# Value tiles as halves: six of eight between the rounds of branch A, two in its sequence, with six value buffers

## The reference, cut to what matters

```python
z = h @ p['w_in']                       # 1024 -> 6944
za = z[..., :SHIFT_W]                   # branch A
zb = z[..., SHIFT_W:SHIFT_W + RET_W]    # branch B: q, k, v, gate
...
def step(S, inp):                       # branch A, token by token
    sk = jnp.einsum('bhvk,bhk->bhv', S, kk_t)
    S = S * w_t[:, :, None, :] - sk[..., None] * b_t[:, :, None, :] + v_t[..., None] * k_t[:, :, None, :]
    return S, jnp.einsum('bhvk,bhk->bhv', S, r_t)
...
q, k, v, gate = jnp.split(zb, [B_QK, 2 * B_QK, 2 * B_QK + B_V], axis=-1)   # v: 8 tiles of 128 columns
```

## Time and profile before

| | |
|---|---|
| runs of the kernel | 1261.36, 1262.67, 1263.44 us; median 1262.67 |
| the profiled execution | 1262.1 us, of it span 1260.3 |
| mean granted TensorE clock | 0.995 |
| PE busy | 1217.3 us (97%), 12056 matmuls |
| PEld, DVE, ACT, POOL busy | 1154.1, 855.5, 558.0, 151.1 us |
| rounds of layer 0 and 1 | 108.3 to 157.8 us, 727.6 to 777.1 us |
| sequence of layer 0 and 1 | 157.8 to 194.5 us, 777.1 to 816.8 us |

### The profile page before, as it was taken

The page is one execution under the profiler, slowest core; times in us unless marked ns, Lnnn a source line. Parts: engine busy times, 40 slices in busy tenths (PEclk is TensorE's granted clock), DMA queues, the critical chain, the costliest instruction groups (busy, mean ns, idle before and its releaser), DMA issues.

```text
span 1260.3 us, 27905 instructions
## 1 busy us (share of the span) xinstructions
PE 1217.3 (97%) x12056; PEld 1154.1 (92%) x12056; DVE 855.5 (68%) x1469; ACT 558.0 (44%) x848; POOL 151.1 (12%) x168
## 2 busy tenths in 40 slices
PE   6999899999999999999999998999999999999996
PEld 5999788999998999999988987889999989999996
DVE  4887558888767766654488965588878576666433
ACT  5553345455445433344354544345463463333432
POOL 0004565100000000000000071920100000000000
PEclk9999999999999999999999999999999999999998
DMA  6433144555453644544434323264544535445441
GB/s 224 137 114 124 55 115 161 200 157 167 135 160 110 207 153 153 149 149 151 150 100 134 120 87 103 73 226 159 161 150 141 161 120 167 150 143 158 149 149 63
DMA packets 51466, 179.13 MB, mean 142 GB/s; under 512 B 6288, under 2 KB 7568, under 8 KB 50064
## 3 DMA queue, kind: packets, MB, share of 16 engines
q1 hardware_dynamic: 42576, 153.77, 39.1%
q10 hardware_dynamic: 8768, 23.58, 5.4%
HBM read 166.18 MB, written 8.53 MB: 139 GB/s over the span
## 4 chain that ended last, share of the span: by engine, by line
PE 86%; DVE 8%; ACT 4%; issue 1%; DMA 0%; ACTq 0%; SPq 0%; DVEq 0%
PE dense L1409 54%; PE core L1409 31%; DVE w_lo L923 2%; ACT w_hi L599 1%; DVE x L983 1%; DVE y_out L981 1%; ACT h_hi L605 1%; DMA x<-x_t 0%; DVE h_lo L1356 0%; DVE bonus L1052 0%; DVE tmp L1038 0%; DVE bonus L1048 0%; ACT sq_mixed L606 0%; PE core L1629 0%; DVE s_ga L1347 0%
## 5 line engine op out<-in xcount | busy, mean ns | idle before, releaser
L923 DVE TENSOR_TENSOR w_lo<-w_raw,w_hi 128x1024 fp32r<-128x1024 f32 x282 | 352.1, 1252 | 215.7 <-ACT w_hi L599 214.7
L599 ACT ACTIVATE w_hi<-w_raw 128x1024 fp32r<-128x1024 f32 x281 | 296.5, 1057 | 429.6 <-PE dense L1409 288.2
L1409 PE MATMUL dense<-h_hi,w_hi 128*128 128x320 f32 x1296 | 413.0, 319 | 16.7 <-DVE w_lo L923 11.7
L1409 PE MATMUL dense<-h_hi,w_lo 128*128 128x320 f32 x1296 | 401.7, 310 | 0.0
L1409 PE MATMUL dense<-h_lo,w_hi 128*128 128x320 f32 x1296 | 396.7, 311 | 0.4 <-DVE h_lo L927 0.4
L1409 PEld LDWEIGHTS dense<-h_hi,w_hi 128*128 128x128 f32 x1296 | 244.8, 189 | 34.9 <-issue 26.5
L1409 PEld LDWEIGHTS dense<-h_lo,w_hi 128*128 128x128 f32 x1296 | 243.3, 189 | 2.7 <-DVE h_lo L927 1.3
L1409 PEld LDWEIGHTS dense<-h_hi,w_lo 128*128 128x128 f32 x1296 | 245.0, 189 | 0.2
L1409 PE MATMUL core<-h_hi,w_hi 128*128 128x320 f32 x416 | 129.1, 310 | 0.5 <-DVE w_lo L923 0.5
L1409 PE MATMUL core<-h_hi,w_lo 128*128 128x320 f32 x416 | 128.5, 309 | 0.0
L1409 PE MATMUL core<-h_lo,w_hi 128*128 128x320 f32 x416 | 128.5, 309 | 0.0
(11 more groups left out here) (307 smaller groups left out, 1987.0 us busy)
## 6 DMA issues: line engine op xcount, KB each, us to landing
w_raw<-wts SPq DMA_DIRECT2D x282, 512.0 KB, 3.5
ret_t<-ret_t ACTq DMA_DIRECT2D x16, 256.0 KB, 4.1
ret_s<-ret_t ACTq DMA_DIRECT2D x16, 256.0 KB, 4.4
ret_rest<-ret_d ACTq DMA_DIRECT2D x2, 1536.0 KB, 8.7
qk_rot<-qk_raw SPq DMA_DIRECT2D x8, 320.0 KB, 6.4
dmask<-rconst ACTq DMA_DIRECT2D x2, 1152.0 KB, 5.5
s_st<-wkv_st ACTq DMA_DIRECT2D x2, 1024.0 KB, 5.0
wkv_s<-s_st ACTq DMA_DIRECT2D x2, 1024.0 KB, 4.2
```

The source lines that it names most:

```text
L599: act.activation(w_hi[n % RING][:, :], w_raw[n % RING][:, :], ACT.Copy).then_inc(hi_ready.sem, 1)
L923: dve.tensor_tensor(w_lo[r][:, :], w_raw[r][:, :], w_hi[r][:, :].bitcast(F32), ALU.subtract).then_inc(low_made.sem, 1)
L1409: return pe.matmul(out, lhsT, rhs, start=start, stop=stop)
```

## The change

Before, four value tiles stand in the rounds, each as three pieces of 3, 3 and 2 blocks, at twelve places; four whole tiles stand in the sequence. After, six tiles stand at the same twelve places as halves of 4 and 4 blocks, and the last two as four halves at the four places of the sequence. All matmuls are the same ones; 48 of them a layer move from the sequence to the rounds. The buffers `v_f` grow from four to six; one lies where `v_tok` begins, so the turns take tile 4 first. The low parts made in the rounds go from four to six, those behind `ys 0`, `ys 1`, `ys 2`, `w 3` from 2, 1, 1, 1 to 1, 1, 0, 1.

```diff
-THIRDS = ((0, 3), (3, 6), (6, 8))
-PIECE_AT = {at: (n // 3, THIRDS[n % 3]) for n, at in enumerate((2, 5, 8, 12, 16, 20, 24, 28, 32, 37, 42, 48))}
-LOW_AT = {10: 1, 18: 2, 30: 3, 42: 4}
+HALVES = ((0, 4), (4, 8))
+PIECE_AT = {at: (n // 2, HALVES[n % 2]) for n, at in enumerate((2, 5, 8, 12, 16, 20, 24, 28, 32, 37, 42, 48))}
+LOW_AT = {6: 1, 13: 2, 21: 3, 29: 4, 37: 5, 45: 6}
...
-FILL_AFTER = {("w", 0): [("turn", 0)], ("u", 0): [("turn", 1)], ("ys", 0): [("tile", 4)], ("w", 1): [("turn", 2)],
...
-LOWS_AFTER = {("ys", 0): (5, 6), ("ys", 1): (7,), ("ys", 2): (8,), ("w", 3): (9,)}
+TURNS = (4, 0, 1, 2, 3, 5, 6, 7)
+FILL_AFTER = {("w", 0): [("turn", 0)], ("u", 0): [("turn", 1)], ("ys", 0): [("half", 12)], ("w", 1): [("turn", 2)],
+              ("u", 1): [("turn", 3)], ("ys", 1): [("half", 13)], ("w", 2): [("turn", 4)], ("ys", 2): [("half", 14)],
+              ("as3", SAMPLE): [("turn", 5)], ("w", 3): [("half", 15)], ("w", SAMPLE): [("turn", 6)], ("u", 3): [("turn", 7)]}
+LOWS_AFTER = {("ys", 0): (7,), ("ys", 1): (8,), ("w", 3): (9,)}
...
-HIGH_AFTER = {("as0", SAMPLE): 4, ("u", 2): 5}
+HIGH_AFTER = {("u", 2): 6}
...
-        v_f = [at("v_f0", 32, T), at("v_f1", 33.25, T), at("v_f2", 34.5, T), at("v_f3", 48, T)]
+        v_f = [at("v_f0", 32, T), at("v_f1", 33.25, T), at("v_f2", 34.5, T), at("v_f3", 124, T),
+               at("v_f4", 38, T), at("v_f5", 48, T)]
...
-                        act.wait_ge(*v_turned(layer, j - T_V - len(v_f) + 1))
+                        act.wait_ge(*v_turned(layer, TURNS.index(j - T_V - len(v_f)) + 1))
...
-                    if h:
-                        pe.wait_ge(*v_tok_ready(layer, h))
+                    if n:
+                        pe.wait_ge(*v_tok_ready(layer, n))
...
-                        if what == "tile":
-                            plain(T_V + i, T_V + i)
+                        if what == "turn":
+                            turn(i)
                         else:
-                            turn(i)
+                            piece(T_V + i // 2, *HALVES[i % 2])
```

More of the change, by code:

```diff
@@ L106 @@
 V_FIRST = max(j for j, _ in PIECE_AT.values()) + 1
-FILL_AFTER = {("w", 0): [("turn", 0)], ("u", 0): [("turn", 1)], ("ys", 0): [("tile", 4)], ("w", 1): [("turn", 2)],
-              ("u", 1): [("turn", 3)], ("ys", 1): [("tile", 5)], ("w", 2): [("turn", 4)], ("ys", 2): [("tile", 6)],
-              ("as3", SAMPLE): [("turn", 5)], ("w", 3): [("tile", 7)], ("w", SAMPLE): [("turn", 6)], ("u", 3): [("turn", 7)]}
-LOWS_AFTER = {("ys", 0): (5, 6), ("ys", 1): (7,), ("ys", 2): (8,), ("w", 3): (9,)}
+TURNS = (4, 0, 1, 2, 3, 5, 6, 7)
[3 more added lines that the diff above has]
+LOWS_AFTER = {("ys", 0): (7,), ("ys", 1): (8,), ("w", 3): (9,)}
 TAIL = [("gate", 0), ("s", 0), ("mean", 0), ("mean", 1), ("s", 1), ("gate", 1), ("s", 2), ("mean", 2), ("mean", 3), ("gate", 2),
@@ L735, in _, with turned_values @@
                         values(T_V + PIECE_AT[i][0])
-                def turned_values(h):
-                    act.wait_ge(*v_turned(layer, h + 1))
+                def turned_values(n):
+                    h = TURNS[n]
+                    act.wait_ge(*v_turned(layer, n + 1))
                     vt = v_tok[:, 0:2048].rearrange("p (b c) -> p b c", b=2)
@@ L767, in _ @@
                     for what, i in FILL_AFTER.get(step, []):
-                        if what == "tile":
-                            values(T_V + i)
-                        else:
+                        if what == "turn":
                             turned_values(i)
+                        elif HALVES[i % 2][1] == KT:
+                            values(T_V + i // 2)
                     if step in HIGH_AFTER:
@@ L1620, in _, with turn @@
                         piece(T_V + PIECE_AT[i][0], *PIECE_AT[i][1])
-                def turn(h):
+                def turn(n):
+                    h = TURNS[n]
                     pe.wait_ge(*v_feat(layer, h + 1))
-                    if h:
-                        pe.wait_ge(*v_tok_ready(layer, h))
+                    if n:
+                        pe.wait_ge(*v_tok_ready(layer, n))
                     f = v_f[h % len(v_f)]
```

## The result

The changed kernel takes 1268.16 us (median of 5 runs, 1264.48 to 1269.09) against 1262.67: a ratio of 1.0041, 95% interval [1.0029, 1.0053]. In a second series on another chip it was 1264.75 us (10 runs, 1262.62 to 1270.45) against 1261.74, ratio 1.0025 [1.0011, 1.0039]. It is slower by 3.0 to 5.5 us; forecast were 6.5 us less, and the time lies outside the range given.

The account below looks back on a forecast made before the run. The prediction took the pace of instruction pages, 3.87 us each, to bound the rounds where pages hold little dense work. Its terms, -3.2 - 3.3 - 0.8 + 0.8 = -6.5 us, gave a median of 1256.2 us, range 1252.5 to 1261.5.

Parts of the forecast that it names:

- Pages bound the rounds: Rounds: where pages of about 126 matmuls hold little dense work, they come every 3.87 us and PE waits for them.
- the rival of no page effect: Rounds: pages aren't the bound and the issue waits stay, so no change, 1262.7 us; chance 0.12.
- The gain of 1.6 us a layer: Rounds of both layers: with 48 matmuls moved in, page waits fall from 3.5 to 1.9 us; -3.2 us for both.
- The late page, -3.3: Layer 1's sequence: the wait for a late instruction page and the half-clock stretch behind it go; -3.3 us.
- The first rival: Sequence of either layer: a page still stands behind the swaps, so the -3.3 is missing, 1259.5 us; chance 0.22.
- "Nothing else": Rest of the kernel: switches stay 16 a layer and the buffers' places add no wait; 0 us, tails included.
- The sequence: Sequence with half the filler: 7.06 us of work leaves each layer's, new waits cost 0.4 us a layer, +0.8 together.
- Waits for DVE: Sequence: up to 0.2 us behind `ys 1` and 0.2 for the samples' `w` copy, 0.4 a layer.
- The wait for `m_sq`: Rounds: PE's 0.4 us wait for ACT's result should be gone; part of the -0.8 us term for result waits.
- The slower rival: Sequences run out of pages: two new late pages besides the old, 3.3 us each, 1266.1 us; chance 0.08.
- the four terms: Page waits in the rounds -3.2, late page -3.3, result waits in the rounds -0.8, sequence with half the filler +0.8 us.

Follow-up runs that it names:

- the small loads: Changed kernel with the weight loads issued within the rounds (tiles 27 to 32 of each layer) bringing 16 rows instead of 128: 1260.00 us, ratio to before 0.9982.
- b_small_loads: Kernel before with the weight loads issued within the rounds (tiles 27 to 30 of each layer) bringing 16 rows instead of 128: 1263.04 us, ratio 1.0002.
- a_again: The changed kernel run once more with nothing altered, for a second profile: ratio 1.0025 to the kernel before.
- a_third: The changed kernel with nothing altered, for a third profile: 1268.31 us, one execution.

## Why the prediction was wrong, step by step

**Pages bound the rounds: right.** The rounds of layer 0 grew by 5.1 us for 7.06 us of moved work, as forecast, and spreading the pieces took further page waits away. PE's own rows show less of it than the sum had: 2.2 us of "issue" in layer 0's rounds now, 2.5 before, where under 2 was forecast, and all its idle time there fell from 3.8 to 2.8 us (49.50 - 45.71, 53.90 - 51.06). The clearest sign is the stops at page ends there, from the last start in one page to the first in the next: those over 0.1 us sum to 3.9 and 4.6 us in the two profiles of the kernel before, and to 2.2 to 2.7 in the four after. The Trainium skill (Runtime: NRT & Kernel Launch, "Instruction fetch mechanics") holds that fetching is hidden. PE's stop of 0.65 us at 762.74, behind a fetch that began 2.6 us late, speaks against it again, so the rival of no page effect falls.

**The gain of 1.6 us a layer: wrong in layer 1, by 2.7 us.** This is the step that failed most clearly. I wrote that the change moves 48 matmuls, and costed these. But a tile that moves into the rounds brings its weight load with it: six loads there instead of four. I had shown the move on SP myself, and counted it only as a gain at the swaps. The loads now come about every 9 us, which is two pages, and in layer 1 in such a phase that every second page is fetched behind one: PE's waits for pages there rose from 2.4 to 3.5 us, where 1.9 was forecast, and fell to 0.9 with the small loads. The page of the earlier trace rows would not have told me, for it comes as late without a full load ahead of it (b_small_loads). What would have is the one fetch of before's rounds that a load did hold, at 773.47 us, 2.7 us late, just as a load of 512 KB ends.

**The late page, -3.3: wrong, by 3.4 us.** Two errors. The 3.3 was one execution's: in the other three profiles with before's order the sequence of layer 1 took 41.8 to 43.0 us, not 44.7, so that the mean of the four has 1 us to give against the shortest, not 3.3. And a stall stayed in three profiles of four. The two loads behind the swaps no longer hold the page, but the last load ahead of them and the swaps themselves now do, and PE comes into the swaps with the page still to be fetched. The first rival had said this, with a chance of 0.22.

**"Nothing else": wrong, 2.8 us in the tails.** I followed what stands behind the swaps on SP, and not who waits for them: POOL's eight rotations, ACT behind these, and then `dmask` on top of the tail's weight load. All of it hangs on the end of the rounds, which now comes 4.4 us further behind their start. About 1.1 of the 2.2 us in layer 0 is the clock drop, in two of the four profiles; in layer 1, a_again and a_third wait 1.2 and 1.0 us for `sq_a`.

**The sequence: right in the sum for layer 0, by luck, since two errors cancel.** Waits for DVE were forecast at 0.4 us a layer. In layer 0 PE now waits 0.8 us for `w_st`, 0.7 for `y_a` behind `ys 1` and 0.5 for `wu_s`, where it waited 0.2 for `w_st` and 0.4 for `v_tok`:

```profile
178.87 0.31 PE L1412 MATMUL dense<-h_hi,w_lo 128*128 128x320 f32 x1
179.86 0.27 PE L1412 MATMUL dense<-v_st,tok 64*64 64x64 f32 x2 [0.68 <-DVE y_a L1170]
```

That is 1.4 us more. Page waits of 0.9 to 1.7 us in the same stretch of the kernel before went to 0.5 and less, which I had not counted. The wait for `m_sq` went, as forecast.

**The slower rival** (three late pages in the sequences, 1266.1) gave nearly the right time by mostly the wrong place. One of its stalls was there.

**The range** was narrower than its own terms. Added up from 1262.7, the bounds of the four terms run from 1250.8 (-7.0, -3.3, -1.6, 0) to 1265.1 us (2.4 for both layers), and not from 1252 to 1261. The 1268.2 us lies above these too, the 1264.75 of the second series just inside.

## What to carry to other kernels

Work that is moved takes its loads along, and what waits for the end of the stretch that it moves into comes later: follow both, through every queue, down to the next engine that PE waits for. Where instruction pages bound a stretch, put bulk transfers right behind the start of a page's fetch rather than ahead of it: in layer 1, four loads in front of fetches cost more here than the page waits that the move should have taken away. And a stall seen in one profile is worth its mean over several, not its size in the one.

## What the runs showed of the hardware that I had not expected

- A page's fetch was not seen to slip into the middle of a load: it began within 0.3 us of the load's end in each of the late cases in layer 1's rounds (751.25 and 751.35; 760.35 and 760.06; 768.76 and 768.83; 777.79 and 777.87), though the packet takes 1 us and the load 2.2. Only close behind a load's start did one begin: at 129.36 in layer 0, 0.6 us behind it, and that load took 3.2 us.
- Two layers with the same instructions came to differ by 2.5 us in the rounds (56.1 and 58.6 us, means of four profiles). Page alignment makes such a difference: with the pages moved by about half, layer 1's rounds fell to 56.1 us. Layer 0's rose to 58.0, in part by a clock drop.
- The same DVE instruction takes over twice the time when a POOL instruction began just ahead of it: `v_exp` 1.05 us in the kernel before, where POOL's first `y_a` (0.88 us from 206.53) runs beside it, and 0.42 after, where POOL is idle. It also took 0.42 at 203.68 after, where POOL began 0.11 us behind it.

```profile
206.64 1.05 DVE L1128 TENSOR_TENSOR v_exp<-v_st,fx 128x256 f32<-128x256 f32 x1
```

```profile
207.91 0.42 DVE L1131 TENSOR_TENSOR v_exp<-v_st,fx 128x256 f32<-128x256 f32 x1
```
